# Rebuilding the token mixer of a hybrid retention / gated linear attention encoder step: head pairs on all 128 partitions, decays inside the rotary tables, x loaded by columns, and the router placed among the next super's steps

## The reference, cut to what matters

```
h = RMSNorm(x)
rq,rk,rv,rg, gq,gk,gv,gg, glr, z_ret, z_gla = split(h @ w_in)      # 4 heads each, keys 64, values 128
retention:  q,k rotated; scores = q k^T * gamma^|n-m| inside a chunk; S = gamma^64 S + (k*decay)^T v
            o = scores v + (q*decay) S_before;  layer norm per head;  times silu(g)
GLA:        log_a = log_sigmoid(glr @ gk2 + b)/16; S = diag(prod a) S + (k*decay)^T v
            o = q S_after;  RMS norm per head;  times silu(g)
m = sigmoid(z_ret)*(o_ret @ w_br_ret) + sigmoid(z_gla)*(o_gla @ w_br_gla)
x = x + m @ w_out
x = x + HierMoE(RMSNorm(x))        # router, then 2 of 32 experts for each row, in blocks of 96 rows
y = RMSNorm(x)
```

## Time and profile before

| | us |
|---|---|
| median of 3 runs | 1685.26 |
| lowest and highest run | 1681.27, 1686.20 |
| span of the profiled execution | 1681.4 |
| of that: up to the first projection | 28.5 |
| projections to the end of the output product, each of three supers | 287.0 to 287.2 |
| from there to the next super's first projection, two times | 30.4 |
| from the last output product to the last router logits | 21.4 |
| routing, experts, last norm | 709.3 |

### The profile page before, as it was taken

One profiled execution on the slowest core, in us unless ns is written; L12 is line 12 of the kernel. 1 busy time (PEld: TensorE's weight loads), 2 busy tenths in 40 slices (PEclk: granted clock), 3 DMA queues, 4 the chain that ended last, 5 costly groups with the idle time before them and its releaser, 6 DMA issues. The chain is left out here.

```text
span 1681.4 us, 25555 instructions
## 1 busy us (share of the span) xinstructions
PE 1519.8 (90%) x8198; PEld 1272.6 (76%) x8198; DVE 1050.2 (62%) x1523; ACT 880.8 (52%) x1187; POOL 352.3 (21%) x492
## 2 busy tenths in 40 slices
PE   6999999999999998999999923999999999999980
PEld 5888899988889998888899912666766666666660
DVE  4665444536644443565444543888988888888863
ACT  4644433355444334644433313777777777777752
POOL 1212111002221110112121022223222222322223
PEclk9999999889999997999999856999999999999995
DMA  6224343322334333224333255999999999999966
GB/s 223 76 89 165 104 139 124 109 96 87 104 141 150 114 101 140 85 83 163 116 113 127 76 178 192 383 374 372 375 382 374 376 378 380 377 373 379 382 214 234
DMA packets 72849, 355.14 MB, mean 211 GB/s; under 512 B 10881, under 2 KB 11154, under 8 KB 48034
## 3 DMA queue, kind: packets, MB, share of 16 engines
q1 hardware_dynamic: 58562, 313.72, 50.6%
q0 software_dynamic: 9824, 25.28, 6.4%
q10 hardware_dynamic: 4368, 14.94, 2.3%
HBM read 326.09 MB, written 28.28 MB: 211 GB/s over the span
## 5 line engine op out<-in xcount | busy, mean ns | idle before, releaser
L1169 DVE TENSOR_TENSOR wlo<-est,whi 128x2048 fp32r<-128x2048 f32 x193 | 440.4, 2290 | 110.9 <-ACT whi L1165 84.1
L1165 ACT ACTIVATE whi<-est 128x2048 fp32r<-128x2048 f32 x193 | 368.4, 1916 | 146.4 <-DMA est<-wexp 104.5
L718 DVE TENSOR_TENSOR w<-stage,w 128x1024 fp32r<-128x1024 f32 x175 | 224.3, 1309 | 79.9 <-ACT w L482 78.1
L482 ACT ACTIVATE w<-stage 128x1024 fp32r<-128x1024 f32 x175 | 178.5, 1054 | 126.4 <-PE ps L959 116.4
L1524 PE MATMUL ps<-whi,xT 128*96 128x512 f32 x512 | 205.6, 401 | 21.7 <-DVE xT L1474 21.7
L1526 PE MATMUL ps<-whi,xT 128*96 128x512 f32 x512 | 203.5, 398 | 0.0
L1525 PE MATMUL ps<-wlo,xT 128*96 128x512 f32 x512 | 202.6, 396 | 0.0
L957 PE MATMUL ps<-w,hT 128*128 128x384 f32 x576 | 199.1, 346 | 0.0
L959 PE MATMUL ps<-w,hT 128*128 128x384 f32 x576 | 193.0, 335 | 0.0
L958 PE MATMUL ps<-w,hT 128*128 128x384 f32 x576 | 192.8, 335 | 0.0
L957 PE MATMUL ps<-hT,w 128*128 128x384 f32 x408 | 141.4, 347 | 8.5 <-issue 5.0
(11 more groups left out here) (214 smaller groups left out, 2754.1 us busy)
## 6 DMA issues: line engine op xcount, KB each, us to landing
est<-wexp SPq DMA_DIRECT2D x193, 1024.0 KB, 13.1
stage<-wmix SPq DMA_DIRECT2D x175, 512.0 KB, 4.2
H<-x_all SPq DMA_DIRECT2D x12, 512.0 KB, 8.2
XR<-x_all SPq DMA_DIRECT2D x9, 512.0 KB, 6.0
x_scratch<-XR ACTq DMA_DIRECT2D x9, 512.0 KB, 5.4
h_scratch<-H ACTq DMA_DIRECT2D x9, 512.0 KB, 6.2
cx<-x_scratch SPq DMA_DIRECT2D x9, 512.0 KB, 7.0
y_all<-co ACTq DMA_DIRECT2D x9, 512.0 KB, 6.2
```

The source lines that it names most:

```text
L482: act.activation(whl[w % 2][0][:, q * PIECE:(q + 1) * PIECE], stage[r % STAGE][:], ACT.Copy)\
L718: vec.tensor_tensor(whl[w % 2][1][o], stage[r % STAGE][:], whl[w % 2][0][o].bitcast(F32), ALU.subtract).then_inc(w_lo, 1)
L1165: act.activation(whi[q][:], est[q][:], ACT.Copy).then_inc(e_hi[q], 1)
L1169: vec.tensor_tensor(wlo[q][:], est[q][:], whi[q][:].bitcast(F32), ALU.subtract).then_inc(e_lo[q], 1)
```

## The change

1. Two heads of a kind form a pair (`PAIRS_H = 4`), whose q, k and states lie on all 128 partitions. A super has 12 pair items and still 24 steps of 24 matmuls: a pair and tile takes its q, k and half of g in one step, and its v and the other half of g in another one, three steps later.
2. The state update and the states' reading are 64 by 64 products in the four quarters of the array, in the order of `ORDER`; a transpose turns both heads. The cleared parts of `kd` are gone.
3. The decays of retention are in the rotary tables (`rotary_tables`, 1.18 MB per super, loaded by SP), so that POOL makes no decayed keys and DVE does not scale and add the two parts of o; both now add up in PSUM.
4. x is loaded by rows for its norm, and by columns (`xT_all`) for the product. PE spreads the row norms over the partitions with one matmul (`spread`), DVE scales the columns (`h_f`), ACT and DVE split them (`h_hi`, `h_lo`). The 24 transposes of x are gone.
5. The router's transposes and logits of super s stand in steps 0 to 3 of super s+1; those of the last super come after it. Nothing is prepared for a super that does not exist.
6. The supers are written out one after the other, without a hardware loop. The output product rotates over four PSUM banks, not two.

```
+PAIRS_H = NHB // 2
+STEPS = 2 * PAIRS_H * TPS
+ITEMS = PAIRS_H * TPS
+        ORDER = [(0, 0), (1, 1), (0, 1), (1, 0)]
...
+            def spread(s):
+                pe.wait_ge(n1_diag, (s + 1) * TPS)
+                pe.matmul(ps[:, 6, 0:TOK], ones_t[:], dg[:, :, :].rearrange("p j n -> p (j n)"), start=True, stop=True)\
+                  .then_inc(rb_mm, 1)
...
+            def updates(s, p, t):
+                for c, h in ORDER:
+                    r = half_of(c)
+                    ins = pe.matmul(ps[half_of(h), B_X + c, 0:HV], rk[r, t, P + h * HK:P + (h + 1) * HK],
+                                    vb[r, t, h * HV:(h + 1) * HV], start=True, stop=True)
+            def read_out(s, p, t):
+                if ret:
+                    for h in range(2):
+                        pe.matmul(ps[:, B_Y + h, 0:HV], sT[:, n % 2, h, :], vb[:, t, h * HV:(h + 1) * HV], start=True, stop=False)
+                for h, c in ORDER:
+                    k = half_of(h)
+                    ins = pe.matmul(ps[half_of(c), B_Y + h, 0:HV], qkT[k, t, c * CHUNK:(c + 1) * CHUNK], st[c][k, :],
+                                    start=not ret, stop=True)
...
-                for i in range(ITEMS + 5):
+                for i in range(STEPS + TAIL):
+                    if s and i < TPS:
+                        h2_turned(s - 1, i, B_X)
+                    if item(i - 1):
+                        turned(s, *item(i - 1))
+                    if item(i - 3) and item(i - 3)[0] < RET_PAIRS:
+                        scores(s, *item(i - 3))
+                    if item(i - 4):
+                        updates(s, *item(i - 4))
+                    if item(i - 5):
+                        read_out(s, *item(i - 5))
+                    if item(i - 7):
+                        o_turned(s, *item(i - 7))
+                    if s and 1 <= i <= TPS:
+                        router(s - 1, i - 1, B_O)
...
+                        if o == 4 and s + 1 < SUPER:
+                            spread(s + 1)
```

DVE at a super's end:

```
-                        for j in range(TPS):
-                            norm1(j, s + 1)
-                for j in range(TPS):
-                    hT_lo_part(j, s + 1)
+                if more:
+                    vec.wait_ge(rb_mm, s + 2)
+                    h_f(s + 1, 0)
+                    for c in range(DC):
+                        if c + 1 < DC:
+                            h_f(s + 1, c + 1)
+                        h_lo(s + 1, c)
+                def h2_rows(j):
+                    vec.wait_ge(out_mm, (s + 1) * OUTS_SB)
```

SP, with the weights of the output product, and DVE in the routing block:

```
+                    if s + 1 < SUPER and r == PIECE0[W_OUT + 2] - 1:
+                        sp.wait_ge(br_mm, (s + 1) * DC)
+                        x_rows(s + 1)
+                        x_columns(s + 1)
...
+            for j in range(TPS):
+                vec.wait_ge(x2_st[j], 16 * SUPER)
+                vec.wait_ge(h2_st[j], 16 * SUPER)
```

More of the change, by code:

```diff
@@ new lines, in build, with item, count, nth @@
+        OUTS_SB = 3 * TPS
+        B_T, B_O, B_X, B_Y = 2, 3, 4, 6
+        OB = [7, 0, 1, 2]
+        ORDER = [(0, 0), (1, 1), (0, 1), (1, 0)]
+        def item(m):
+            if 0 <= m < STEPS and m % (2 * TPS) < TPS:
+                return m // (2 * TPS), m % (2 * TPS)
+            return None
+        def count(m, most):
+            if m < 0:
+                return 0
+            return min(m // (2 * TPS) * TPS + min(m % (2 * TPS) + 1, TPS), most)
+        def nth(s, p, t):
+            return (s * PAIRS_H + p) * TPS + t
@@ L953, in _ @@
+                x2_sum(2, 1)
+                x2_sum(2, 2)
+                for j in range(TPS):
+                    if more:
+                        split_lo(s + 1, 1, j)
+                    h2_rows(j)
+            for j in range(TPS):
+                log_sum(SUPER - 1, j, j % 2)
         @block.tensor
@@ new lines, in x_free, with scores @@
+            def x_free(s, i):
+                if s * ITEMS + count(i - 5, ITEMS):
+                    pe.wait_ge(s_upd, s * ITEMS + count(i - 5, ITEMS))
+                if s * RET_ITEMS + count(i - 4, RET_ITEMS):
+                    pe.wait_ge(sT_cp, s * RET_ITEMS + count(i - 4, RET_ITEMS))
+                if s:
+                    pe.wait_ge(n2_cp, s * TPS)
+            def scores(s, p, t):
+                n = nth(s, p, t)
+                pe.wait_ge(qkT_cp, n + 1)
+                for h in range(2):
+                    k = half_of(h)
+                    ins = pe.matmul(ps[:, B_X + h, P:2 * P], qkT[k, t, P:2 * P], qkT[k, t, 0:P], start=True, stop=True)
+                ins.then_inc(score, 1)
@@ new lines, in h2_turned, with router @@
+            def h2_turned(s, j, bank):
+                pe.wait_ge(n2_h, s * TPS + j + 1)
+                for c in range(DC):
+                    ins = pe.transpose(ps[:, bank + c // 4, (c % 4) * P:(c % 4 + 1) * P], h2[j][:, c * P:(c + 1) * P], ident)
+                ins.then_inc(n2_tr, 1)
+            def router(s, j, bank):
+                pe.wait_ge(n2_cp, s * TPS + j + 1)
+                for c in range(DC):
+                    ins = pe.matmul(ps[:, bank, 0:36], h2T[:, j * D + c * P:j * D + (c + 1) * P], wr[:, c, :],
+                                    start=(c == 0), stop=(c == DC - 1))
+                ins.then_inc(log_mm, 1)
@@ new lines, in _, with out_chunks @@
+                z_part(s, 1, 0)
+                br_part(s, 0)
+                z_part(s, 1, 1)
+                br_part(s, 1)
+                for d in range(2, DC):
+                    z_part(s, d, 0)
+                    z_part(s, d, 1)
+                    br_part(s, d)
+                def out_chunks(n, j, first, end):
+                    c0, cn = OUT_COLS[n]
+                    W = weights(W_OUT + n, cn)
+                    for c in range(first, end):
+                        if j == 0:
+                            weights_in(s, W_OUT + n, cn, c)
+                        ins = three(ps[:, OB[(n * TPS + j) % 4], 0:cn], mT, W, (A3, c, slice(j * P, (j + 1) * P)),
+                                    (A3, c, A3), c == 0, c == DC - 1)
+                    return ins
```

1349 lines of the change are left out of this document (700 added, 649 removed).

## The result

The changed kernel takes 1568.22 us (median of four runs, 1566.86 to 1571.97); the kernel before, beside it, 1685.73 (1681.27 to 1687.44). The ratio is 0.9311, 95% interval 0.9294 to 0.9328: 117.5 us less, where I had forecast 81.5.

The account below looks back on a forecast made before the run. PE was taken to bound the supers; small products -45, gaps -50.2, router +18.2 and smaller terms sum to -81.5 from the profiled 1681.4 us: 1599.9, plus 3.9 for the median, rounded 1604 us. Range 1578 to 1638, 8 in 10.

Parts of the forecast that it names:

- Small products: PE's small matmuls in the supers: 64 by 64 passes two at a time, 15 us saved a super, -45 for three.
- rival (b): Small matmuls in the supers: all four quarters of the array work at once, -18, 1585; chance 0.14.
- The gaps: Between supers: low-rank product follows the output product at full clock, 5.3 us in place of 30.4; -50.2 for two.
- chain at B + 15 and B + 34: Before the gap: B ends the branch products; x is wanted near B+15, h ready at B+32.6, ahead of B+34.7.
- rival (c): Between supers: x, its scaling or the pieces come late, each gap 17 us in place of 5.3: +23, 1627; chance 0.13.
- The router in the steps: Router transposes and logits moved into the steps of two supers cost PE 9.1 us each: +18.2.
- The start: First projection step waits for eight MB of transfers and ends at 29 in place of 32.7: -3.7, bounds -7 and 0.
- The end: Last router logits come 16.7 us after the output product in place of 21.35: -4.6; -9 with the full clock.
- New waits: In steps heavier for DVE and ACT, or in the tail: 1.5 us a super, +4.5, bounds 0 and 12.
- (a): Small matmuls in the supers: the 64 by 64 products run one after the other, +32, 1635; chance 0.13.
- (d): Written-out mixer: instruction fetches hold PE up, slower than before, past 1685 (1712 at 1.2 us a fetch); chance 0.03.
- (e): In the supers: DVE takes PE's place as the bound, no gain, the time stays at 1685; chance 0.01.

Follow-up runs that it names:

- e_one_quarter: Changed kernel with twelve more 64 by 64 matmuls in each update group, all on the first quarter of the array: 1662.72 us.
- e_router_behind: Changed kernel with every super's router transposes and logits put back behind its own output product, not in the next super's steps: 1595.59 us.
- e_start3: Start of e_start2 in the changed kernel, with the fourth weight piece loaded ahead of parameters, other constants and rotary table: 1566.73 us.
- e_order_rows: Changed kernel with the four quarters in another order, so that neighbours in the order share the array's rows: 1568.0 us.
- e_four_rounds: Changed kernel with each update group issued four times over its four quarters instead of once: 1592.67 us.
- e_before_written_out: Kernel before the change with only the mixer's loop over supers written out on all five engines: 1680.55 us against 1685.49.
- e_copy_mid: Changed kernel with the update group of 33 of 36 pairs issued once more, amid the large products of its step: 1587.07 us.
- e_start2: Changed kernel with only identity and norm weights loaded ahead of x's rows, the other constants behind the first pieces: 1568.95 us.
- e_better2: Changed kernel with scores times v issued ahead of the scores, together with the start of e_start2: 1568.16 us.

## Why the prediction was wrong, point by point

**Small products: the step that failed.** I wrote "with the 64 by 64 passes again two at a time (0.05 each)". Four run at a time, 0.028 each. The prices measured:

| | forecast | measured |
|---|---|---|
| pass on a quarter, four in use | 0.05 | 0.028 |
| pass on a quarter, one in use | 0.105 | 0.109 |
| pass on half the rows, two in use | 0.105 | 0.058 |
| change of kind | 0.19 | 0.17 |

A pass costs 0.11 us times the share of the array that it takes, when the rest is in use. With these prices my own counts give 0.14 + 0.23 + 0.22 + 0.42 + 0.22 + 0.14 + 6.7 x 0.17 = 2.5 for a retention pair and 0.65 + 3.7 x 0.17 = 1.28 for a GLA pair; the trace has 2.5 and 1.26. The first super's stretch is 23.3 shorter, where spreading (+0.6) and gates (-0.7) cancel, so three supers give -70 in place of -45. Of the 25, 24 are these: 576 passes on quarters x 0.022 = 12.7; 72 score passes x 0.047 = 3.4; 187 changes x 0.02 = 3.7; and 4.3 because I took 2.3 and 1.4 where a head's small products took 2.37 and 1.45 (with 4.17 for the large products). The 4.17 was in reach: I had divided the whole stretch by 23 and got 0.177 a start, but only the first start-to-start in it, 0.25 from 100.72 behind the small products, is longer and belongs to the change of kind; the others are 0.174.

```profile
100.97 0.34 PE L958 MATMUL ps<-w,hT 128*128 128x384 f32 x1
101.15 0.34 PE L959 MATMUL ps<-w,hT 128*128 128x384 f32 x1
```

How I missed it: I read the update's full price in the earlier trace rows as evidence against quarters. But those passes take all 128 rows, and both write to the same 64 partitions, so that they stand on the same half of the array; and passes on one and the same part follow each other at the full price (0.109, e_one_quarter). The row could say nothing of quarters. The rows that bore on the question were the states' reading, which showed two quarters 10 ns apart. I held it for a pair and stopped there. It was rival (b), to which I gave 0.14. Its price, -18, was right: quarters and scores came to 12.7 + 3.4 = 16.1. The Trainium skill (TensorE: Matmul & The Clock Gate, Packing small matmuls) states that such matmuls run side by side with about 4 ns between starts. The runs agree in size: by that rule, as an estimate, four passes end 0.012 after one, 0.109 + 0.012 = 0.121, and four rounds gave 4 x 0.028 = 0.113. The starts themselves lie some 10 ns apart in the trace. The other rule that I weighed (TensorEngine Tiling (Array Packing), Key Properties: a change of mode drains the engine, a change of tile does not) holds too: 0.17 for a change of mode, and nothing for the order of the tiles. The fixed part between update and transposes in the earlier trace rows, where the shape stays the same, it does not cover.

**The gaps: right.** 4.18 with the clock at 1.00, forecast 5.3. The 1.1 us of waits that I had added were a slip: a third piece ready at +7.5 and wanted at +6.9 is 0.6 late, and that lies inside the first projection step, not in the gap; there it measured 0.37. The chain at B + 15 and B + 34 held; rival (c) did not come. That much of it hangs on the router's place is shown by e_router_behind.

**The router in the steps: right**, 7.8 a super in place of 9.1. ACT is no releaser.

**The start: the size right, the reason wrong.** The first projection came 3.0 earlier and step 0 ended at 30.0 (29 forecast). I had eight MB as the bound. e_start3 ends step 0 at 27.05 with the same transfers in another order, so that my sum of bytes came near by luck.

**The end:** 13.6, forecast 16.7. I had 6.4 until the router starts and three times 3.45 at the half level. It starts 6.0 behind the output product, and takes 7.43 for all 48 passes: the clock falls only while it runs (1.00 in the window of the transposes, 0.71 in that of the router). This 13.6 is one value of several. The same instructions behind the same waits took 11.7 in the profile of e_order_rows (router 5.45, clock 1.00) and 15.1 in that of e_start3 (8.83, 0.59); in eight of the fifteen profiles of the changed kernel and its variants the router took 5.4 to 5.5. The -9 that I gave for the full clock is that case. What decides when the clock falls there is open.

**New waits: too many.** I had 4.5. The whole of the supers' difference, -54.7, against -70 + 15.6 + 1.3 - 2 leaves 0.4. That is a remainder, as the -70 and the 15.6 are themselves read from whole stretches; the idle time of PE says the same: the old stretches had 1.8 each, and the new have 1.5 to 1.7.

**The other rivals.** (a) fell with e_four_rounds. (d) fell with e_before_written_out: written out, the old kernel is 4.9 faster. (e) fell: DVE is busy for 132 of 264.

**The range.** Its low end stood on rival (b) alone, as if only one term could be wrong. Rival (b) came true and gave 16 of the 36 us. Changes (3.7), the large products' spacing (4.3), router (2.6), waits (4.1), gaps (2.3) and end (3.1) all came out on the cheap side too, and together they gave the other 20 and carried the time below the range. I had bounds for several of these terms and never added up what they would be if they all lay on one side.

## What to carry to other kernels

When matmuls are smaller than the array, price a pass by the share of rows times columns that it takes, and ask of each row of the old trace whether its neighbours could have overlapped at all before reading its price as a rule. What is left is the number of changes between tile shapes: order the small products of a step so that one shape follows itself, since 24 fewer changes were 4 us here for nothing. And a small piece of work that fits between full-rate matmuls costs its own time there (7.8 us for a router), but two to three times that where PE waits for its operands and its clock is down (20 and 23 us a gap in e_router_behind).

## What was not expected of the hardware

- A change of tile shape is not paid in one place: 0.10 ahead of the small group, some 0.16 behind it (0.38 less eight passes), and 0.10 more between the next two large products (e_copy_mid). A reading of start-to-start times that stops at the next instruction misses the last piece.
- The order of quarters makes no difference, not even where two in a row share all their rows (e_order_rows: 1568.0 against 1568.2).
- In e_router_behind the same transposes and router took 11.7 us behind the last output product and 17.8 behind the first (24.6 less 6.85 for the low-rank product). The idle time of PE ahead of them was 1.71 in the one and 3.75 in the other, and the granted clock 1.00 throughout in the one, 0.52 and 0.71 in the other. Two microseconds more of waiting went with six more in all.
- The granted clock after such a wait is not the same from case to case: behind 2.91 us of idle time in e_start2 it was at half for about 3 us, behind 2.59 in e_better2 for about 9, although PE was busy all the while. At the mixer's end the same 48 router passes took 5.4 to 8.8 us.
- Same code, same data, other time: routing and experts took 709.3 to 716.1 in the profiles, more than most edits here are worth. What moves it is open.
